# The cumulative sums of a stick-breaking attention: full-precision products, or two rounded passes each

## The reference, cut to what matters

```
z = (q . k) * dh**-0.5                       # per head, query t, key s
log_fail = where(s < t, log_sigmoid(-z), 0)
after = reverse_cumsum(log_fail, keys) - log_fail
a = where(s < t, exp(log_sigmoid(z) + after), 0)
out = a @ v
```

## Time and profile before

| | |
|---|---|
| median of the runs | 1565.62 us |
| span of the profiled execution | 1562.4 us; its own time is not listed beside it, the median of the timed runs is 3.2 above |
| TensorE busy, its granted clock | 98%; full in all 40 slices to the tenth |
| VectorE, ScalarE, GpSimd busy | 57%, 48%, 17% |
| the four pairs | from about 965 to 1112 us of the span |
| chain that ended last | 90% TensorE, 5% VectorE, 3% ScalarE |

### The profile page before, as it was taken

One profiled execution on the slowest core, in us unless ns is written; L12 is line 12 of the kernel. 1 busy time (PEld: TensorE's weight loads), 2 busy tenths in 40 slices (PEclk: granted clock), 3 DMA queues, 4 the chain that ended last, 5 costly groups with the idle time before them and its releaser, 6 DMA issues.

```text
span 1562.4 us, 20671 instructions
## 1 busy us (share of the span) xinstructions
PE 1531.7 (98%) x7650; PEld 1222.0 (78%) x7650; DVE 893.4 (57%) x1681; ACT 751.1 (48%) x1310; POOL 258.1 (17%) x453
## 2 busy tenths in 40 slices
PE   9989999999999999999998999999999999999998
PEld 7878888888878777777776887666678888888877
DVE  5767677776656456666666435554375243443476
ACT  4454455544553346666667314656555241332343
POOL 1033323443313003343343000000000000000000
PEclk9999999999999999999999999999999999999999
DMA  5311111211114332222222231112222223233221
GB/s 202 109 54 54 55 54 55 67 55 55 47 48 153 99 106 73 84 82 68 81 76 68 81 108 63 54 68 68 67 85 91 94 95 108 84 105 95 94 95 54
DMA packets 40163, 127.22 MB, mean 81 GB/s; under 512 B 4576, under 2 KB 9104, under 8 KB 40064
## 3 DMA queue, kind: packets, MB, share of 16 engines
q1 hardware_dynamic: 38112, 121.65, 24.1%
q0 software_dynamic: 1040, 3.27, 0.6%
q10 hardware_dynamic: 912, 0.99, 0.2%
HBM read 122.69 MB, written 2.15 MB: 80 GB/s over the span
## 4 chain that ended last, share of the span: by engine, by line
PE 90%; DVE 5%; ACT 3%; POOL 1%; issue 1%; DMA 0%; SPq 0%; POOLq 0%; ACTq 0%; DVEq 0%
PE ps L833 87%; PE ps L1196 2%; PE ps L976 1%; DVE wl L1945 1%; ACT L L1751 1%; POOL L L2761 1%; DVE h L2595 1%; DVE mo L2589 1%; POOL uc L2731 0%; POOL masks L2729 0%; DVE L L2452 0%; DVE up L2080 0%; DMA wraw<-in_wa 0%; DVE xm L2582 0%; ACT wh L1340 0%
## 5 line engine op out<-in xcount | busy, mean ns | idle before, releaser
L833 PE MATMUL ps<-xr,wh 128*128 128x512 f32 x2752 | 880.1, 401 | 3.5 <-DVE xr L2388 1.2
L833 PEld LDWEIGHTS ps<-xr,wh 128*128 128x128 f32 x2752 | 505.7, 188 | 129.6 <-issue 30.5
L833 PE MATMUL ps<-xr,wl 128*128 128x512 f32 x1376 | 538.4, 391 | 0.0
L1945 DVE TENSOR_TENSOR wl<-wraw,wh 128x1024 fp32r<-128x1024 f32 x214 | 264.5, 1243 | 130.9 <-ACT wh L1340 128.8
L833 PEld LDWEIGHTS ps<-xr,wl 128*128 128x128 f32 x1376 | 258.6, 188 | 56.1
L1340 ACT ACTIVATE wh<-wraw 128x1024 fp32r<-128x1024 f32 x214 | 222.2, 1049 | 85.8 <-PE ps L833 83.8
L833 PE MATMUL ps<-xm,wh 128*128 128x512 f32 x640 | 198.8, 392 | 5.1 <-DVE xm L2582 2.7
L833 PEld LDWEIGHTS ps<-xm,wh 128*128 128x128 f32 x640 | 119.5, 188 | 33.5 <-DVE xm L2582 4.0
L2761 POOL TENSOR_SCALAR L<-L,m 128x256 f32<-128x256 f32 (+1 forms) x128 | 99.2, 794 | 272.2 <-DVE m L2467 272.2
L833 PE MATMUL ps<-xm,wl 128*128 128x512 f32 x320 | 124.7, 390 | 0.0
L1983 DVE SCALAR_TENSOR_TENSOR qkv<-cin,gains,qkv 128x512 f32<-128x512 f32 x96 | 77.3, 807 | 10.6 <-ACT qkv L1370 9.7
(11 more groups left out here) (265 smaller groups left out, 1749.7 us busy)
## 6 DMA issues: line engine op xcount, KB each, us to landing
wraw<-in_wa SPq DMA_DIRECT2D x48, 512.0 KB, 3.7
wraw<-in_wb SPq DMA_DIRECT2D x32, 512.0 KB, 4.0
wraw<-in_wu SPq DMA_DIRECT2D x32, 512.0 KB, 3.6
wraw<-in_wd SPq DMA_DIRECT2D x32, 512.0 KB, 3.7
wraw<-in_wao SPq DMA_DIRECT2D x16, 512.0 KB, 3.7
wraw<-in_wbo SPq DMA_DIRECT2D x16, 512.0 KB, 3.9
wraw<-in_wc SPq DMA_DIRECT2D x16, 512.0 KB, 3.7
bias<-rel_rows SPq DMA_DIRECT2D x16, 256.0 KB, 3.8
```

What stands on the lines that cost most here:

```text
L833: return e.matmul(out, w, x, start=start, stop=stop, skip_group_check=True)
L1945: e.tensor_tensor(m.wl[:, i % N_SPLIT, :], m.raw[:, i % N_RAW, :], m.wh[:, i % N_SPLIT, :].bitcast(F), ALU.subtract).then_inc(s.wlo, 1)
```

## The change

For pairs 0 to 2 (`SPLIT_PAIRS = 3`) the operands of W are split like the weights: a high part rounded by ScalarE (hi3 to hi0 for `sp`, hs2 and hs1 for the sums) and a low part by GpSimd (lo and ls), subtracted in place or into freed space. Each product of W becomes two rounded passes against a rounded copy of the triangle and of the ones, which ScalarE makes once. Pair 3 keeps full precision. VectorE's sums move up, from the W steps to right behind M, and W waits for M alone. The order tables c0 to c2 are new. `sp` is laid out in 1152 columns for a head in place of 1536, and the new tiles lie in it, in unused slices of `XR` and over `sqt`, `rb` and `rt`, for which ScalarE waits for the norm factor before it loads mask and `wpool`. Some semaphores of loads are merged.

```diff
-    "c0": plan("x0 s0 s7 s8 s0 s0 s11 s0 s2 s3 s0 s0 s1 s0 s2"),
-    "c1": plan("s0 s6 s5 x2 s0 s11 s0 s0 s0 s6 s0 s0 s0 s1 s5"),
-    "c2": plan("x1 s0 s8 s4 s3 s5 s0 s0 s5 s2 s0 s0 s1 s0 s6"),
+    "c0": plan("x0 s0 s7 s7 s0 s0 s8 s0 s4 s5 s0 s1 s1 s0 s1"),
+    "c1": plan("s0 s7 s5 x2 s0 s9 s0 s0 s0 s9 s0 s1 s0 s1 s2"),
+    "c2": plan("x1 s0 s7 s7 s0 s8 s0 s0 s4 s5 s0 s1 s1 s0 s1"),
...
# tensor_program, stick
+        def weights_split(i):
+            ntri, nones = m.tri[:, 0, :], m.tri[:, 1, :]
...
+            for he in range(2):
+                if i == 2:
+                    later = m.stick(m.sph, he, 3), m.stick(m.spl, he, 3)
+                elif i < 2:
+                    later = ((m.sum1h, m.sum1l), (m.sum2h, m.sum2l))[i]
+                    later = later[0][:, he], later[1][:, he]
+                    e.wait_ge(s.st_a[he], stick_a(j, f"hs{i + 1}"))
+                    e.wait_ge(s.st_o[he], stick_o(j, f"ls{i + 1}"))
+                if i < 3:
+                    e.wait_ge(s.st_v[he], stick_v(j, f"M{i}"))
+                    mm(z(i, he)[:, 128:], nones, later[0], False, False)
+                    mm(z(i, he)[:, 128:], nones, later[1], False, False)
+            for he in range(2):
+                e.wait_ge(s.st_a[he], stick_a(j, f"hi{i}"))
+                mm(z(i, he), ntri, m.stick(m.sph, he, i), False, False)
+            for he in range(2):
+                e.wait_ge(s.st_o[he], stick_o(j, f"lo{i}"))
+                mm(z(i, he), ntri, m.stick(m.spl, he, i), False, True).then_inc(s.st_p[he], 1)
...
# scalar_program, stick
+        def high(i):
+            e.wait_ge(s.st_v[ee], stick_v(j, f"M{i}"))
+            if i == 1:
+                e.wait_ge(s.st_p[ee], stick_p(j, "W2"))
+            did(e.activation(m.stick(m.sph, ee, i), m.stick(m.sp, ee, i), ACT.Copy))
+            if i in (1, 2):
+                whole, hi = ((m.sum1, m.sum1h), (m.sum2, m.sum2h))[i - 1]
+                e.wait_ge(s.st_v[ee], stick_v(j, f"U{i}b"))
+                did(e.activation(hi[:, ee], whole[:, ee], ACT.Copy))
+
         def logits(i):
...
+            if i == 2 and j < SPLIT_PAIRS:
+                high(3)
...
         def weights(i):
+            if i and j < SPLIT_PAIRS:
+                high(i - 1)
...
# pool_program, stick (step 0 of head 0)
+        def low(i):
+            for he in range(2):
+                e.wait_ge(s.st_a[he], stick_a(j, f"hi{i}"))
+                e.wait_ge(s.st_v[he], stick_v(j, ("M0", "U1b", "U2b", "C3")[i]))
+                e.tensor_tensor(m.stick(m.spl, he, i), m.stick(m.sp, he, i), m.stick(m.sph, he, i).bitcast(F),
+                                ALU.subtract).then_inc(s.st_o[he], 1)
...
+            low(3)
+            for i in (2, 1):
+                low(i)
+                low_sum(i)
+            low(0)
```

More of the change, by code:

```diff
@@ L612, in __init__ @@
         self.vc = c.new([2, 4, 3, 64], name="vc")
-        self.sp = c.new([2, 3, 512], name="sp")
+        poff = c.p
+        self.sp = c.new([2, 1152], name="sp")
+        self.spl = at(poff, [2, 1152], R, "spl")
+        self.sph = c.new([2, 896], R, "sph")
         self.am = c.new([2, 2, 512], name="am")
-        self.spsum = c.new([2, 512], name="spsum")
+        self.sum2 = c.new([2, 256], name="sum")
+        self.sum2h = self.XR[:, 23, :].rearrange("p (e c) -> p e c", e=2)
+        self.sum2l = self.XR[:, 31, :].rearrange("p (e c) -> p e c", e=2)
+        self.sum1h = at(soff, [2, 384], R, "sumh")
+        self.sum1, self.sum1l = at(soff + 3 * KB, [2, 384], F, "sum"), at(soff + 3 * KB, [2, 384], R, "suml")
+        self.tri = at(roff, [2, 128], R, "tri")
+        self.smask = at(roff + KB, [128], F, "smask")
         self.yt = c.new([2, 512], name="yt")
@@ L681, in __init__ @@
         self.xres = [new(f"xres{k}") for k in range(8)]
-        self.flip, self.rel, self.hot, self.neg, self.sinks = (new(n) for n in ("flip", "rel", "hot", "neg", "sinks"))
+        self.flip, self.rel, self.neg = (new(n) for n in ("flip_sinks", "rel_hot", "neg"))
         self.rows = new("rel_rows_written")
@@ L729, in __init__ @@
         self.ct_p, self.cvt = new("cv_turned"), new("cv_kept")
-        self.st_p, self.st_a, self.st_v = ([new(f"stick_{n}{e}") for e in range(2)] for n in ("pe", "act", "dve"))
+        self.st_p, self.st_a, self.st_v, self.st_o = (
+            [new(f"stick_{n}{e}") for e in range(2)] for n in ("pe", "act", "dve", "pool"))
         self.y_p, self.y_a, self.y_v = new("y_pe"), new("y_act"), new("y_dve")
@@ L758 @@
     ("L3", "L2", "W3", "L1", "W2", "V3", "L0", "W1", "V2", "W0", "V1", "V0"))}
+SPLIT_PAIRS = 3
+STICK_A_SPLIT = {"ln3": 3, "hi3": 4, "ln2": 7, "hi2": 8, "hs2": 9, "x3": 10, "ln1": 13, "hi1": 14, "hs1": 15, "x2": 16,
+                 "ln0": 19, "hi0": 20, "x1": 21, "x0": 22}
 STICK_A = {"ln3": 3, "ln2": 6, "x3": 7, "ln1": 10, "x2": 11, "ln0": 14, "x1": 15, "x0": 16}
-STICK_V = {n: i + 1 for i, n in enumerate(("K3", "M3", "K2", "M2", "C3", "K1", "M1", "U2a", "U2b", "K0", "M0", "U1a", "U1b"))}
+STICK_V = {n: i + 1 for i, n in enumerate(("K3", "M3", "C3", "K2", "M2", "U2a", "U2b", "K1", "M1", "U1a", "U1b", "K0", "M0"))}
+STICK_O = {n: i + 1 for i, n in enumerate(("lo3", "lo2", "ls2", "lo1", "ls1", "lo0"))}
 POOL_BASE = (21, 15, 8, 0)
@@ L2770, in begin_c, with stick, low_sum @@
             e.memset(x, 0.0).then_inc(s.cz, 1)
+    @part
+    def stick(j, ee):
+        def low(i):
[4 more added lines that the diff above has]
+                                ALU.subtract).then_inc(s.st_o[he], 1)
+        def low_sum(i):
+            whole, hi, lo = ((m.sum1, m.sum1h, m.sum1l), (m.sum2, m.sum2h, m.sum2l))[i - 1]
+            for he in range(2):
+                e.wait_ge(s.st_a[he], stick_a(j, f"hs{i}"))
+                e.tensor_tensor(lo[:, he], whole[:, he], hi[:, he].bitcast(F), ALU.subtract).then_inc(s.st_o[he], 1)
+        if ee == 0 and j < SPLIT_PAIRS:
+            low(3)
[3 more added lines that the diff above has]
+            low(0)
+        yield
     @part
```

81 lines of the change are left out of this document (45 added, 36 removed).

## The result

The changed kernel takes 1582.89 us (median of 5 runs, 1580.51 to 1585.41); the kernel before, on the same chip, 1565.62 (1563.91 to 1569.04). The ratio is 1.0102, 95% interval 1.0086 to 1.0119. Forecast was 1568.8, with 1560 to 1573.5 for 8 in 10: right that it gets slower, but by 17.3 us between the medians (16.0 by the ratio) and not 3.2. The profiled run of after is one of the slower ones, 1585.41 us with a span of 1583.6.

The account below looks back on a forecast made before the run. TensorE, busy 98% of the span, was taken as the bound. Its saving of 8.8 us and 0.5 at pair 3, against added waits of 4.5, 0.7, 1.5, 1.2, 2.5 and 2.1, gave +3.2: 1568.8 us, 8-in-10 range 1560 to 1573.5.

Parts of the forecast that it names:

- Saved on TensorE: Cumulative sums W of pairs 0 to 2: 7.05 us a pair becomes 4.11 in rounded passes, -8.8 us for three.
- W3: Cumulative sum of block 3, first in a pair: TensorE waits 1.5 us for head 1's copy and subtraction, +4.5 for three.
- one sign that I had set for a wrong forecast: TensorE at W3: the forecast is wrong if no wait over 0.5 us there is released by GpSimd.
- L0: Logits of block 0 in pair 0: bank cleared later, as copies precede x2 on ScalarE; +0.7 us, from 0 to 1.5.
- GpSimd beside VectorE: Last GpSimd subtraction before W0 runs longer beside VectorE: 0.4 us a pair, +1.2, from 0 to 2.
- W0: Cumulative sum of block 0, last in a pair: its last operand comes late; 0.5 us each, +1.5.
- From pair to pair: New tables leave fewer product steps between a pair's y and the next L3: +2.5 and +2.1 us, 1 to 5 together.
- K3 of pair 3: Sign at the mask on pair 3's block 3 logits: it would start four us or more behind its L3.
- The clock: Rival: waits of 2 to 3 us make TensorE's clock fall, 1.7 us each, two falls, 1572 us; chance 0.12.
- a drop between 960 and 1110 us: Sign over the four head pairs: the forecast is wrong if the granted clock drops there.

Follow-up runs that it names:

- e6: Changed kernel with every GpSimd subtraction cut to 4 columns and the low passes fed the high tile; 1569.7 us.
- e14: Changed kernel with the 12 low parts of a pair subtracted on VectorE instead of GpSimd; 1571.5 us.
- e2: Changed kernel with no pair split (full precision in all four), new order tables kept; 1570.8 us.
- e3: Changed kernel with no pair split and the old order tables; 1565.6 us, ratio 0.9993 to the kernel before.
- e5: Changed kernel with W3 and the 128-column ones' product of W2 back in full precision, without hi3 and lo3; 1579.1 us.
- e11: Changed kernel with old order tables and only W0 split in pairs 0 to 2, low parts on GpSimd; 1567.7 us.
- e12: Changed kernel with old order tables and only W0 split, its low parts subtracted on VectorE; 1564.3 us, ratio 0.9980 to the kernel before.
- e7: Changed kernel with 14 unused rounded matmuls of 256 columns between the two high passes of W3 in each split pair; 1583.8 us.
- e8: e5 with other order tables: more steps between M1 and W1 and between L3 and W0, pair 3's approach filled as before; 1576.5 us.
- e9: e6 with 36 full-width GpSimd subtractions on other data added behind the short ones; 1578.0 us.
- e15: e12 with W1 split as well, low parts on VectorE; 1567.5 us, ratio 0.9999 to the kernel before.
- e1: Changed kernel with order tables c0 to c2 of the kernel before, split kept; 1577.7 us.
- e13: Changed kernel with ScalarE's x3 and x2 moved ahead of the copies hi2, hs2 and hi1, hs1; 1581.3 us.
- e10: e6 with extra 4-column GpSimd subtractions as a pause ahead of each short low part; 1590.0 us.

## Why the prediction was wrong

**Saved on TensorE: 6.7 for 8.8.** The passes were priced right: 0.11, 0.12 and 0.17 us for 128, 256 and 384 columns. Left out was what it costs to come to another width or operand, 0.05 us or so at each such place: a pair's four W take 4.65 and not 4.11 us. And pair 0's 7.05 us before were taken for all three pairs, where pair 2's are 6.54.

**W3: the mechanism right, 6.4 for 4.5.** hi3 of head 1 behind Ln2 of head 0, as written, with waits of 2.2, 1.5 and 1.9 for 1.5 each, and 0.26 more between the two low passes, for GpSimd. The sum had the subtraction behind the copy for 0.46; what TensorE waits for is the copy, ahead of the second high pass. So one sign that I had set for a wrong forecast came: there is no wait over 0.5 us at W3 that GpSimd ends.

**L0: 3.0 for 0.7, outside its bounds of 0 to 1.5.** TensorE came to L0 when it was forecast to (22.3 us behind the first L3); x2 came 2.1 us later than forecast. 1.7 of it is that I took Ln1's end from the kernel before. In after Ln1 of head 1 ends 994.71 - 972.26 = 22.45 us behind the first L3, where it was 20.75, since K1 stands on VectorE behind the pool group's additions at L2144, and these ran beside GpSimd's subtractions; in e6, where they don't, Ln1 is 0.4 late. The three additions before and after, and GpSimd at that time:

```profile
978.18 2.14 DVE L2080 TENSOR_TENSOR up<-up 128x512 f32<-128x512 f32 x3
```

```profile
985.10 0.69 DVE L2137 TENSOR_TENSOR up<-ps,rb 128x512 f32<-128x512 f32 x1
985.90 3.22 DVE L2144 TENSOR_TENSOR up<-up 128x512 f32<-128x512 f32 x3
```

```profile
984.66 1.64 POOL L2842 TENSOR_TENSOR spl<-sp,sph 128x256 fp32r<-128x256 f32 x2 [3.30 <-ACT sph L1886]
986.25 2.32 POOL L2849 TENSOR_TENSOR xr<-sum,xr 128x256 fp32r<-128x256 f32 x2
```

The other 0.4 is that I counted ScalarE's copies and left out what hs1 waits for: hs1 of head 1 waits for sum1's addition, and this ran beside GpSimd's lo1 of head 0. VectorE, ScalarE and GpSimd in pair 0 of after:

```profile
994.09 0.62 ACT L1905 ACTIVATE sp<-sp,k 128x384 f32<-128x384 f32 x1
...
996.65 0.52 ACT L1890 ACTIVATE sumh<-sum 128x384 fp32r<-128x384 f32 x1 [0.43 <-DVE sum L2605]
```

```profile
995.33 1.14 DVE L2604 TENSOR_TENSOR sum<-sum,sp 128x256 f32<-128x256 f32 x1
```

```profile
995.20 1.00 POOL L2842 TENSOR_TENSOR spl<-sp,sph 128x384 fp32r<-128x384 f32 x1 [6.63 <-ACT sph L1886]
```

The addition took 1.14 us in place of 0.42 and ended 0.27 behind GpSimd's end, then the copy, x2, and L0.

**GpSimd beside VectorE: the step that failed.** I priced it at 1.2 us as a longer lo0. The slow row of GpSimd has another side: an operation of VectorE with two SBUF inputs waits as well. The additions at L2144 took 0.69 us alone and 1.10 beside GpSimd's 1.18, ending 0.55 behind each GpSimd operation: the engines take turns. In the stretch that is 10 us of VectorE's time (85.4 busy in after, 75.5 in e6, which has the same instructions on it), ahead of M, K and the weight splits. With the waits and the half-clock time that hang on it, the low parts cost 12.1 us more on GpSimd than on VectorE (e14), and 13.7 more than as good as none (e6). The Trainium skill (SBUF — State Buffer, "SBUF: two separate sides") has the rule as an exclusive lock for the whole instruction, taken by whichever starts first. The trace agrees, with the 0.55 us above. By that rule VectorE loses as well as GpSimd; I had priced GpSimd's side alone.

**W0: 3.3 for 1.5 plus 1.2.** About right in sum, but unevenly: 0.3, 1.6, 1.5, and about a third of it for M0 and not for GpSimd.

**From pair to pair: 3.6 for 4.6, and the tables alone cost 4.9 to 6.0 (e2).** The wait of 3.0 came in a projection product ahead of L3, whose bank VectorE emptied late (L2122), and not at W3 of pair 3. TensorE from y of pair 2 to L3 of pair 3 took the same 6.9 us as before, with three steps in it for eight. K3 of pair 3 started 0.8 us behind its L3 and not four or more, since the wait came ahead of L3.

**The clock: a term that the sum had at nothing.** I had set it beside the waits as another way to go, a rival at 12%, and a drop between 960 and 1110 us as a sign that the forecast is wrong. It comes with the waits. In the profiles there is none at half clock in before, e3, e5, e11 and e12, 3.4 to 6.8 us in e2, e6, e7, e8, e9, e14 and e15, 13.6 in after and in e1, 17.0 in e13, and 23.8 in e10, where every W0 has a wait of 2.1 us or more. It added 6.3 us to after's stretch, and 9.2 us to after's time over all runs, the largest part of the miss. e5 (as many waits of 2 to 3 us at logits, full clock in its profile) and e8 (the same kind, 6.8) show that a wait doesn't always bring it; which ones do is left open.

**Terms added as if independent.** e5, e13 and e8 took waits away and got most of them back downstream within the pair. My W3 and L0 terms were in part two readings of one lateness. What is left of the 16.0 to 17.3 us beside the stretch is 2 to 3 us, and the 9.2 us by the clock are 2.9 more than the 6.3 in the stretch: this part is half-clock time outside the four pairs, and what brings it there isn't shown.

## What to carry to other kernels

Before work goes to an idle GpSimd, look at what VectorE does at that time: where it reads two SBUF operands, each engine stopped for the other here, and the cost was on the chain of the busier one. When TensorE's work in a chain of dependent steps is cut, ask what the chain through the other engines gets longer by; cut first where the chain is touched least (here the last step, W0, with its low parts on VectorE). And put a price on the clock for each wait that is added, not beside them.

## What the runs showed of the hardware

VectorE additions and subtractions with both inputs in SBUF took 0.42 us (256 columns) and 0.69 (512) alone, 1.14 and 1.10 to 1.5 beside a GpSimd subtraction of 384 or 256 columns. Two SBUF inputs aren't the whole of it: the copy of 128 columns at L2598, with one, took 0.22 us alone and 0.47 beside a GpSimd subtraction. Operations with one input in PSUM kept their time: the product at L2137 took 0.69 us at 985.10, beside GpSimd, and 0.69 alone. GpSimd subtractions of 4 columns, 168 of them in a row or nearly, took 0.28 us on the mean and stretched nothing on VectorE (e10).

```profile
978.55 0.47 DVE L2598 COPY sum<-sp 128x128 f32<-128x128 f32 x1
```

In W3 the four records of full precision took 0.36 us before, and the four rounded passes of 128 columns take 0.55 without their wait: at 128 columns the split saves nothing.

The time at half clock differed between executions of one kernel, from 0 to 22 us for the kernel before and from 25 to 38 for after. The span less half of it differed by much less: its standard deviation over 81 runs of the kernel before is 1.0 us.
